# Attention in pairs of cached units behind each head's full products, and two key units loaded early into the room of the spread sample probabilities

## What is computed

```python
# prompt: 8 heads, 256 queries over 256 keys, causal, with a slope per head on the distance
# sample: 8 sequences of 8 queries over 256 cached keys (two pages of 128) and their own 8 new ones
s = einsum('bqhd,bqhnkd->bqhnk', q, k) * scale - slope[h] * dist
p = softmax(where(ok & (dist >= 0), s, -inf))
out = einsum('bqhnk,bqhnkd->bqhd', p, v)        # heads of 128
# k_past = cache_k[page_table], v_past = cache_v[page_table], 8 heads x 128 values per key
```

## Time and profile before

| | us |
|---|---|
| median of 3 runs (lowest to highest) | 1246.15 (1245.74 to 1247.38) |
| span of the profiled execution | 1245.6 |
| PE busy | 1234.8 (99%) |
| DVE busy | 727.1 (58%) |
| ACT busy | 580.6 (47%) |
| POOL busy | 80.7 (6%) |
| attention, 939.2 to 974.0 of the span: PE busy | 34.69 of 34.80 |

### The profile page before, as it was taken

One profiled execution on the slowest core, in us unless ns is written; L12 is line 12 of the kernel. 1 busy time (PEld: TensorE's weight loads), 2 busy tenths in 40 slices (PEclk: granted clock), 3 DMA queues, 4 the chain that ended last, 5 costly groups with the idle time before them and its releaser, 6 DMA issues.

```text
span 1245.6 us, 21960 instructions
## 1 busy us (share of the span) xinstructions
PE 1234.8 (99%) x8827; PEld 1210.0 (97%) x8827; DVE 727.1 (58%) x1125; ACT 580.6 (47%) x931; POOL 80.7 (6%) x99
## 2 busy tenths in 40 slices
PE   8999999999999999999999999999999999999997
PEld 8999999989999999999998999999997999999997
DVE  6655655575777656554564655654567485655443
ACT  5534333454556445443445554433444464544332
POOL 0000001100332000000000000000020110000010
PEclk9999999999999999999999999999999999999998
DMA  9344344533444443334544744334578734443441
GB/s 338 138 147 156 105 138 150 206 131 137 136 160 148 160 164 135 136 117 144 194 152 147 251 138 165 124 116 145 188 269 307 273 135 154 149 142 119 140 139 42
DMA packets 35465, 200.40 MB, mean 161 GB/s; under 512 B 4234, under 2 KB 4618, under 8 KB 20178
## 3 DMA queue, kind: packets, MB, share of 16 engines
q1 hardware_dynamic: 33426, 192.27, 44.3%
q0 software_dynamic: 1984, 7.38, 1.9%
HBM read 193.06 MB, written 6.57 MB: 160 GB/s over the span
## 4 chain that ended last, share of the span: by engine, by line
PE 99%; DVE 0%; DMA 0%; ACT 0%; SPq 0%; issue 0%; DVEq 0%; ACTq 0%
PE bank L514 30%; PE bank L516 29%; PE bank L515 29%; PE bank L663 1%; PE bank L664 1%; PE bank L662 1%; PE bank L994 1%; PE bank L665 1%; PE bank L666 1%; PE bank L819 0%; PE bank L954 0%; DMA x<-x_in 0%; PE bank L774 0%; PE bank L922 0%; PE bank L912 0%; PE bank L904 0%
## 5 line engine op out<-in xcount | busy, mean ns | idle before, releaser
L514 PE MATMUL bank<-h_hi,w_hi 128*128 128x320 f32 x1792 | 557.0, 311 | 2.2 <-DVE h_lo L1535 2.2
L516 PE MATMUL bank<-h_hi,w_lo 128*128 128x320 f32 x1792 | 555.4, 310 | 0.0
L515 PE MATMUL bank<-h_lo,w_hi 128*128 128x320 f32 x1792 | 555.3, 310 | 0.0
L1107 ACT ACTIVATE w_hi<-raw 128x1024 fp32r<-128x1024 f32 (+1 forms) x364 | 331.9, 958 | 443.3 <-PE bank L516 423.0
L1521 DVE TENSOR_TENSOR w_lo<-raw,w_hi 128x1024 fp32r<-128x1024 f32 (+1 forms) x364 | 388.5, 1107 | 133.6 <-ACT w_hi L1107 133.6
L514 PEld LDWEIGHTS bank<-h_hi,w_hi 128*128 128x128 f32 x1792 | 337.3, 188 | 3.7 <-issue 2.6
L515 PEld LDWEIGHTS bank<-h_lo,w_hi 128*128 128x128 f32 x1792 | 337.2, 188 | 0.1
L516 PEld LDWEIGHTS bank<-h_hi,w_lo 128*128 128x128 f32 x1792 | 337.2, 188 | 0.0
L516 PE MATMUL bank<-f_hi,w_lo 128*128 128x320 f32 x704 | 217.6, 309 | 0.0
L514 PE MATMUL bank<-f_hi,w_hi 128*128 128x320 f32 x704 | 217.6, 309 | 0.0
L515 PE MATMUL bank<-f_lo,w_hi 128*128 128x320 f32 x704 | 217.6, 309 | 0.0
(11 more groups left out here) (252 smaller groups left out, 757.9 us busy)
## 6 DMA issues: line engine op xcount, KB each, us to landing
raw<-w_in SPq DMA_DIRECT2D x86, 1024.0 KB, 4.8
raw<-w_out SPq DMA_DIRECT2D x64, 704.0 KB, 4.1
raw<-w_a SPq DMA_DIRECT2D x12, 1024.0 KB, 4.8
raw<-w_kv SPq DMA_DIRECT2D x8, 1024.0 KB, 4.8
raw<-vc_in SPq DMA_DIRECT2D x12, 512.0 KB, 7.1
raw<-kc_in SPq DMA_DIRECT2D x10, 512.0 KB, 4.4
raw<-w_oa SPq DMA_DIRECT2D x4, 1024.0 KB, 5.5
raw<-w_q SPq DMA_DIRECT2D x4, 1024.0 KB, 4.8
```

The costliest lines, as they stand in the source:

```text
L514: pe.matmul(out, wh, mh, start=first, stop=False)
L515: pe.matmul(out, wh, ml, start=False, stop=False)
L516: return pe.matmul(out, wl, mh, start=False, stop=last)
L1107: sc.activation(w_hi[:, n_at % 2, part * w:part * w + w], raw[:, raw_of(n_at) % RAW, part * w:part * w + w], ACT.Copy).then_inc(hi_done, 1)
```

## The change

PE's list in the attention has another order. Units 1, 2, 3 follow each other behind `prompt_scores(1)`. From there on a head's full-array steps stand together and the packed units stand behind them, mostly in twos (`UNITS_BEHIND`): outputs h - 1, scores h + 2, turn h, then the units. `prompt_turn(7)` and `prompt_outputs(6)` follow unit 15, as they did before. The transpositions of the sample's probabilities stand together ahead of heads 2 and 4. ACT makes `prompt_hi` one head later, behind the next head's copy, and DVE `prompt_lo` behind the next bias. Two more cache units, 0 and 1, are loaded into rooms, which are the first 4096 of 5120 columns of `p_spread`; GpSimd zeroes these columns only when unit 1 has been used, and `spread_probs` waits for that.

```diff
+        p_room = p_spread[:, :, :, :, :].rearrange("p a r k x -> p (a r k x)")
         rooms = [... the three rooms of before,
+                 [p_room[:, 0:1024], p_room[:, 1024:2048]], [p_room[:, 2048:3072], p_room[:, 3072:4096]]]
-        CACHE, EARLY = 2 * NB, 3
-        ROOM = {4: 0, 5: 1, 6: 2, NB + 3: 0, NB + 4: 1}
+        CACHE, EARLY = 2 * NB, 5
+        ROOM = {4: 0, 5: 1, 6: 2, NB + 3: 0, NB + 4: 1, 0: 3, 1: 4}
+        UNITS_BEHIND = ((4, 5), (6, 7), (8, 9), (10, 11), (12, 13), (14,), (15,))
 # SP
             load_room(5, 1)
+            load_room(0, 0)
+            load_room(0, 1)
+            load_room(1, 0)
+            load_room(1, 1)
             load_room(6, 0)
-            load_cache(0)
+            load_cache(2)
             sp.wait_ge(rms_done, 5)
             load_room(6, 1)
-            for c in range(1, CACHE):
+            for c in range(3, CACHE):
 # PE: turn_probs(i) becomes turn_new_probs(i) (one transposition) and turn_page_probs(i) (two)
             cache_unit(1)
+            cache_unit(2)
+            cache_unit(3)
             for h in range(H - 1):
-                if h == 1:
-                    pe.wait_ge(qa_sp, 4)
-                cache_unit(2 * h + 2)
                 if h in (2, 4):
-                    turn_probs(h - 1)
-                if h == 0:
-                    cache_unit(3)
-                prompt_turn(h)
+                    turn_new_probs(h - 2)
+                    turn_new_probs(h - 1)
+                    turn_page_probs(h - 2)
+                    turn_page_probs(h - 1)
+                if h >= 1:
+                    prompt_outputs(h - 1)
+                if h == H - 2:
+                    turn_early_outputs()
                 if h + 2 < H:
                     prompt_scores(h + 2)
-                if h > 0:
-                    cache_unit(2 * h + 3)
-                if h == H - 2:
-                    prompt_turn(H - 1)
-                prompt_outputs(h)
-                if h in (1, 3):
-                    turn_probs(h - 1)
-                if h == 5:
-                    turn_early_outputs()
+                prompt_turn(h)
+                if h == 0:
+                    pe.wait_ge(qa_sp, 4)
+                for c in UNITS_BEHIND[h]:
+                    cache_unit(c)
+            prompt_turn(H - 1)
+            prompt_outputs(H - 2)
 # ACT, loop over h from 0 to 6, behind prompt_copy(h) and the sample's exponentials
-                if h < H - 2:
-                    prompt_hi(h)
+                if h >= 1:
+                    prompt_hi(h - 1)
 # DVE
-            ve.wait_ge(spread_set, 3)
+            ve.wait_ge(spread_set, 1)
 # spread_probs
+                ve.wait_ge(spread_set, 4)
                 ve.wait_ge(sm_t, i + 1)
 # loop over h from 0 to 7
                 prompt_probs(h)
-                if 1 <= h < H - 1:
-                    prompt_lo(h - 1)
...
                 if h + 2 < H:
                     prompt_bias(h + 2)
+                if 1 <= h < H - 1:
+                    prompt_lo(h - 1)
 # GpSimd
             gp.memset(q_spread[:, :, :, :], 0.0).then_inc(spread_set, 1)
-            gp.memset(p_spread[:, :, :, :, :], 0.0).then_inc(spread_set, 1)
             gp.memset(p_new[:, :, :], 0.0).then_inc(spread_set, 1)
+            gp.memset(p_room[:, 4096:5120], 0.0).then_inc(spread_set, 1)
+
+            gp.wait_ge(kv_used, 2)
+            gp.memset(p_room[:, 0:4096], 0.0).then_inc(spread_set, 1)
             add_squares(5)
```

More of the change, by code:

```diff
@@ L168, in trunk_program @@
                 sst = sb("sst", [128, 3, 4], f32, own)
+        p_room = p_spread[:, :, :, :, :].rearrange("p a r k x -> p (a r k x)")
         rooms = [[page_k[:, 0:1024], page_k[:, 1024:2048]], [keys_room[:, 0:1024], keys_room[:, 1024:2048]],
-                      [row_room[:, 0:1024], norm_room[:, 0:1024]]]
+                 [row_room[:, 0:1024], norm_room[:, 0:1024]],
+                 [p_room[:, 0:1024], p_room[:, 1024:2048]], [p_room[:, 2048:3072], p_room[:, 3072:4096]]]
         ident, ones = con[:, C_ID:C_ID + 128], ones_r[:, :].bitcast(f32)
@@ L958, in cache_scores, with turn_new_probs, turn_page_probs @@
                     mm.then_inc(kv_used, 1)
-            def turn_probs(i):
+            def turn_new_probs(i):
                 r = ORDER[i]
                 pe.wait_ge(sm_e, i + 1)
+                w = SLOT * (r % 2) + SLOT
+                pe.transpose(bank[r][0:w, 256:384], ss[:, r, PAST + SLOT - w:PAST + SLOT], ident)
+            def turn_page_probs(i):
+                r = ORDER[i]
                 for pg in range(NPG):
-                    pe.transpose(bank[r][:, pg * 128:pg * 128 + 128], ss[:, r, pg * PAGE:pg * PAGE + PAGE], ident)
-                w = SLOT * (r % 2) + SLOT
-                pe.transpose(bank[r][0:w, 256:384], ss[:, r, PAST + SLOT - w:PAST + SLOT], ident).then_inc(sm_t, 1)
+                    mm = pe.transpose(bank[r][:, pg * 128:pg * 128 + 128], ss[:, r, pg * PAGE:pg * PAGE + PAGE], ident)
+                mm.then_inc(sm_t, 1)
             def cache_outputs(b):
```

## The result

The changed kernel took 1249.91 us in the median of 7 runs, 1246.15 before; ratio 1.0024, 95% interval 1.0015 to 1.0033. Timed again it took 1250.06 against 1246.96, ratio 1.0024 (1.0013 to 1.0035). It is slower by 0.24%. I had forecast 1246.7 in a range of 1244.5 to 1248.4: wrong. The ratios in this document leave out two disturbed executions, one of the kernel with the rooms only (6485 us) and one of the kernel before (1503 us).

The account below looks back on a forecast made before the run. PE, busy 99% of the span, was taken as the bound. New waits 2.25, less 1.49 for fewer visits and 0.26 for old waits gone, gave +0.5 on 1246.15: 1246.7 us, range 1244.5 to 1248.4.

Parts of the forecast that it names:

- The visits: PE in the attention: switches from full-array steps to packed units and back fall from 14 to 9, saving 1.49 us.
- Rival 5: Packed units on PE: loss is paid per unit, not per visit, so only waits count; +2.0, 1248.1 us, chance 0.04.
- The waits that come: PE in the attention: four new waits on steps queued in ACT and DVE, together 2.25 us.
- (a): Turn 7 behind unit 15: PE waits 1.01 us for the chain through ACT and DVE.
- (b): Outputs 5 behind unit 14: PE waits 0.68 us for the low part of head 4, queued behind head 7's bias.
- (c): Unit 12: PE waits 0.50 us for the second pair of spreads; 0.1 at the first pair's pace.
- (d): Unit 8: PE waits 0.06 us for the first pair of spreads, up to 0.5 at the second pair's pace.
- Rival 2: Attention: the new waits don't come, only the savings count; -1.8, 1244.4 us, chance 0.22.
- Rival 4: PE's clock falls behind the wait at turn 7; +2.3, 1248.4 us, chance 0.06.
- The later memset: GpSimd zeroes 4096 columns from about 943 to 946.5, hidden; price on DVE taken as 0, between 0 and 2.1 us.
- Rival 3: The memset holds DVE beside the scalings of heads 0 and 1; +2.1 on the forecast, +2.6, 1248.8 us, chance 0.06.
- The early loads: Two more cache units loaded ahead of the attention: worth nothing, since PE never waited for a landing there.

Follow-up runs that it names:

- control: The kernel before, unchanged, run once more against itself; ratio 1.0003 (0.9994 to 1.0012), attention 34.84 us.

## Why the prediction was wrong

The sum was +0.5; the attention grew by 1.96, and 0.4 came around the span, by the medians.

1. **The visits, saved 1.49: right.** Full removal of the waits left -1.46 against before, with two gaps left, 0.3 in all. Rival 5 is out: two units together take 1.86 instead of 2 x 1.01.
2. **The waits that come, 2.25: right in sum.** (a) 1.01 forecast, 1.03 measured (2.04 - 1.01); (b) 0.68 and 0.85; (c) 0.50 and 0.49; (d) 0.06 and 0; together 2.37. With the memset out of the way the attention takes 35.29, +0.45 where I had +0.5. Rival 2 is out, and the earlier high and low parts show that these waits are the loop that I had named. Rival 4 is out too: behind wait (a), from 974 to 985, the granted clock is 1.00.
3. **The later memset, priced at nothing: this is the step that failed.** It costs 1.51 (36.80 - 35.29). I had both ends, 0 and +2.1, and chose 0 by the reciprocals of the earlier trace rows, which aren't the form in question. No row of before showed a scaling of one SBUF input beside a memset, so the nearest row was not near. The first scaling took 3.35 us instead of 0.29, as at the upper end. The scalings ended 2.9 us late (3.48 instead of 0.55). PE, whose scores were through at 944.69 (944.26 + 0.43), stood until 946.15: 1.46, so the slack was 1.5, where I had taken 1.4. The price is under my 2.1 mainly because the scalings' own 0.55 lies inside the memset. Rival 3 had the mechanism and should have had far more than 0.06: the sentence of the Trainium skill was all that I had on that form, and it pointed that way.
4. **The early loads, worth nothing: wrong, but hidden.** I argued from a PE that had never waited for a landing. That was so at the old pace. At the new one, without them, it waits, and the attention is 0.87 us longer in the order of the change, 1.57 with the parts earlier. In the order of the change they earned less than their own memset cost: 36.80 with both, 36.16 without.
5. **"Around the span doesn't change": wrong.** It is 1.7 to 1.9 us for the kernel before and its control, in every execution whose span is on record. For each kernel with other code its median is 2.0 to 2.2, even for the ones that are no slower. Single executions go further: all 22 of the two kernels without the early loads have 2.0 to 2.1, but of 65 executions of the kernels with them 15 have 2.8 to 4.1, three of seven in each timing of the changed kernel. What it is, no run shows.

Steps 3 and 5 took the time out of the range: +0.5 had become +1.96, and with the 0.4 it is +2.4, which is 1248.5. By the means around the span, 2.6 and 2.7 against 1.8, it is +2.8 to +2.9. The measured medians are +3.8 and +3.1 (means +3.4 and +2.6). They hold the start of the program besides, which moves a run by 2 us, and its end, which moves it by up to 1.6; how much of the +3.8 is either can't be told, since for the first seven runs of before no spans are on record. I also took the median of three runs of before and one profiled span as if 0.55 between them were fixed. By the 1.8 of all others, the profiled execution took about 1247.4, the highest of the three.

No version is measurably quicker than before: the lowest ratios are 0.9994 and twice 0.9996, and all three intervals hold 1. One of the 0.9996 belongs to a kernel whose attention is 0.59 us longer than before, so these ratios don't rank the versions. The trace of the best says -1.46 us in the attention, 0.12%, of which the 0.25 around the span goes off again.

## What to carry to other kernels

When a GpSimd instruction is moved, look at what DVE does at its new place, form by form: in this kernel a long memset there held a quick one-input DVE instruction to its end. Cut it into pieces whose hold fits into the slack, or use a DVE form that isn't held. A prefetch that covers no wait today may cover one at the pace that the rest of the change makes, so try each half without the other. And where several short loops run through in-order queues, a part that is ready early should stand ahead of one that waits for later work.

## What the runs showed of the hardware

A DVE tensor_scalar fp32 of 128x128 in SBUF took 3345 ns beside a memset of 3511 ns and 286 ns otherwise; a tensor_tensor with two SBUF inputs beside the same memset took at most 421. A memset that found such tensor_scalars under way took 0.21 to 0.23 us longer than its neighbours.

In thirteen traces the attention starts at 938.33 to 940.62, and from PE's 200th matmul (35.0 to 37.2 us) to that point every one of them takes 903.4 us. What differs is the start of the program: none to 20 matmuls over 320 columns there start 0.27 us apart instead of 0.15 (none in the changed kernel's first trace, 12 in that of before), and PE's idle time varies by 0.9. The granted clock of the profile doesn't always show such matmuls: from 5 to 30 us it is 1.00 in the first trace with the high and low part earlier, which has 18 of them. From the first matmul of the output product to the end, the same code takes 270.7 to 272.3 us.
